# A two-block transformer kernel on one core: w_ada's chunks dealt anew between TensorE and VectorE, filler multiplications of a constant tile in three pauses, and the attention's quotient moved behind its last product

## The reference

```
mod = silu(c) @ w_ada + b_ada                       # 2048 x 12288, one row
shift_a, scale_a, gate_a, shift_f, scale_f, gate_f = split(mod, 6)
h = rms_norm(x, g_attn_pre) * (1 + scale_a) + shift_a
proj = h @ w_in                                     # 2048 x 5456
diff = (softmax(q1 k1) - lam * softmax(q2 k2)) v, then rms_norm     # 8 heads
dsa  = softmax over each query's 64 best keys, chosen by an indexer # 8 heads
x = x + gate_a * rms_norm(concat(diff, dsa) @ w_o, g_attn_post)
h = rms_norm(x, g_ffn_pre) * (1 + scale_f) + shift_f
x = x + gate_f * rms_norm((silu(h @ w_gate) * (h @ w_up)) @ w_down, g_ffn_post)
# second block: latent attention and a gated convolution on w_in_2, then
x = x + rms_norm(merged @ w_out_2, post_norm_g_2)
```

## Time and profile before

| | us |
|---|---|
| median of 3 executions | 2359.15 (2357.89 to 2360.88) |
| profiled execution | 2358.56 |
| its span in the trace | 2357.3 |
| PE busy | 2279.3 (97%) |
| DVE busy | 1401.9 (59%) |
| ACT busy | 1070.8 (45%) |
| mean DMA rate | 215 GB/s |

### The profile page before, as it was taken

One profiled execution on the slowest core, in us unless ns is written; L12 is line 12 of the kernel. 1 busy time (PEld: TensorE's weight loads), 2 busy tenths in 40 slices (PEclk: granted clock), 3 DMA queues, 4 the chain that ended last, 5 costly groups with the idle time before them and its releaser, 6 DMA issues.

```text
span 2357.3 us, 26193 instructions
## 1 busy us (share of the span) xinstructions
PE 2279.3 (97%) x10706; PEld 1843.9 (78%) x10706; DVE 1401.9 (59%) x1902; ACT 1070.8 (45%) x1481; POOL 0.7 (0%) x5
## 2 busy tenths in 40 slices
PE   6989899989999999999999999999999999999998
PEld 3666677778888888888887878888888888888887
DVE  3669999786774555455456554545544554554555
ACT  2424455544434444434445555555444444444443
POOL 0000000000000000000000000000000000000000
PEclk9999999999999999999999999999999999999999
DMA  9887667665775665555553644444555555555553
GB/s 401 342 349 290 261 259 283 242 252 194 290 276 203 220 226 192 183 196 196 181 194 113 249 153 156 158 159 164 187 192 194 191 184 196 183 192 195 181 192 146
DMA packets 79548, 507.77 MB, mean 215 GB/s; under 512 B 8364, under 2 KB 18860, under 8 KB 19780
## 3 DMA queue, kind: packets, MB, share of 16 engines
q1 hardware_dynamic: 79428, 506.10, 58.5%
HBM read 501.87 MB, written 4.19 MB: 215 GB/s over the span
## 4 chain that ended last, share of the span: by engine, by line
PE 88%; DVE 6%; ACT 2%; DMA 2%; issue 1%; SPq 0%; DVEq 0%; ACTq 0%
PE bank L611 27%; PE bank L613 27%; PE bank L612 27%; DMA raw<-in_chunks_dram 2%; PE bank L656 1%; DVE wlo L1787 1%; PE bank L741 1%; DVE acc L1768 1%; PE bank L575 1%; ACT whi L1133 1%; PE bank L664 1%; PE bank L764 0%; DVE P L1946 0%; PE bank L744 0%; DVE x L1848 0%
## 5 line engine op out<-in xcount | busy, mean ns | idle before, releaser
L1787 DVE TENSOR_TENSOR wlo<-raw,whi 128x1024 fp32r<-128x1024 f32 (+2 forms) x760 | 912.5, 1204 | 837.6 <-ACT whi L1133 836.2
L1133 ACT ACTIVATE whi<-raw 128x1024 fp32r<-128x1024 f32 (+2 forms) x760 | 790.0, 1044 | 1002.2 <-PE bank L613 910.4
L611 PE MATMUL bank<-whi,Ahi 128*128 128x512 f32 (+2 forms) x2304 | 909.0, 395 | 31.1 <-DVE wlo L1787 21.0
L613 PE MATMUL bank<-whi,Alo 128*128 128x512 f32 (+2 forms) x2304 | 893.8, 388 | 0.0
L612 PE MATMUL bank<-wlo,Ahi 128*128 128x512 f32 (+2 forms) x2304 | 893.7, 388 | 0.0
L611 PEld LDWEIGHTS bank<-whi,Ahi 128*128 128x128 f32 x2304 | 435.5, 189 | 138.0 <-DVE wlo L1787 31.3
L613 PEld LDWEIGHTS bank<-whi,Alo 128*128 128x128 f32 x2304 | 435.4, 189 | 89.4
L612 PEld LDWEIGHTS bank<-wlo,Ahi 128*128 128x128 f32 x2304 | 436.1, 189 | 82.3
L1768 DVE SCALAR_TENSOR_TENSOR acc<-raw,cs,acc 128x512 f32<-128x512 f32 x224 | 157.4, 744 | 0.1
L611 PE MATMUL bank<-whi,Fhi 128*128 128x512 f32 x352 | 137.6, 391 | 0.0
L613 PE MATMUL bank<-whi,Flo 128*128 128x512 f32 x352 | 137.1, 389 | 0.0
(11 more groups left out here) (292 smaller groups left out, 1336.9 us busy)
## 6 DMA issues: line engine op xcount, KB each, us to landing
raw<-in_chunks_dram SPq DMA_DIRECT2D x456, 1024.0 KB, 4.8
raw<-in_chunks_dram SPq DMA_DIRECT2D x8, 768.0 KB, 4.2
raw<-in_chunks_dram SPq DMA_DIRECT2D x8, 576.0 KB, 4.1
raw<-in_chunks_dram SPq DMA_DIRECT2D x4, 672.0 KB, 8.1
x<-in_x_turned_dram SPq DMA_DIRECT2D x2, 1024.0 KB, 10.3
x<-in_x_dram SPq DMA_DIRECT2D x4, 512.0 KB, 5.8
x_spill<-x SPq DMA_DIRECT2D x2, 1024.0 KB, 9.7
x<-x_spill SPq DMA_DIRECT2D x2, 1024.0 KB, 8.9
```

The source lines that it names most:

```text
L611: pe.matmul(o, a_hi, w_hi, start=beg and kk == 0, stop=False)
L613: ins = pe.matmul(o, a_lo, w_hi, start=False, stop=fin and kk == 1)
L1133: act.activation(m.whi[:, i % NHL, :, 0:n], m.raw[:, c % NRAW, 2 * h:2 * h + 2, 0:n], ACT.Copy).then_inc(m.s_hi, 1)
L1787: dve.tensor_tensor(m.wlo[:, i % NHL, :, 0:n], m.raw[:, c % NRAW, 2 * h:2 * h + 2, 0:n], m.whi[:, i % NHL, :, 0:n].bitcast(F32), ALU.subtr ...
```

## The change

It has four parts. (1) `ADA_ON_PE` loses groups 1, 2 and 3, the shifts of quarters 1 to 3; VectorE multiplies them, at the head of its own list. TensorE has 20 chunks, VectorE 60 up to the end of `w_o`. (2) The deal: TensorE's chunks follow the first two passes of each of three quarters; VectorE's are spread over all quarters, and `W_IN_HALF` sets how many fall in each half of `W_IN_ORDER`. The shift of the next quarter now comes by `ada_take` in bank 5; banks 6 and 7 alternate for the scales. `idle` is only set after quarter 2. (3) `keep_busy(b, n)` multiplies a tile of ones with the constants, 440 columns, n times, into a bank that nobody reads: at the start, and in both `turn_halves`, ahead of each wait. (4) `combine` makes `E1 - lam * s1 / s2 * E2`, and ScalarE multiplies with 1 / s1 as it copies the product out, in one instruction for each half of the positions.

```diff
--- before.py
+++ after.py
@@ -38,15 +38,16 @@
 W_IN_ORDER = (4, 6, 1, 3, 5, 7)
 
 
-DEAL_PE = ((3, 3, 2, 2, 1), (2, 2, 1, 1, 1), (2, 2, 2, 0, 0), (0, 0, 0, 0, 0))
-DEAL_VECTOR = ((0, 0, 0, 0, 0), (0, 0, 0, 1, 1), (0, 0, 0, 1, 1), (1, 1, 1, 1, 2))
-W_IN_SHARE = 24
+DEAL_PE = ((2, 2, 0, 0, 0), (2, 2, 0, 0, 0), (2, 2, 0, 0, 0), (0, 0, 0, 0, 0))
+DEAL_VECTOR = ((0, 2, 2, 1, 1), (0, 1, 1, 1, 1), (0, 1, 1, 1, 1), (1, 0, 1, 1, 1))
+
+W_IN_HALF, W_IN_SHARE = 11, 25
 W_O_SHARE = 15
 THIRDS = ((0, 4), (4, 8), (8, 11))
 
 
 
-ADA_ON_PE = (4, 0, 5, 1, 6, 2, 7, 3)
+ADA_ON_PE = (4, 0, 5, 6, 7)
 
 
 def win_cols(cg):
@@ -61,7 +62,7 @@
         plan.append(("lin", w, k0, c0, n))
 
     first = [("ada", g, j) for g in ADA_ON_PE for j in range(4)]
-    rest = [("ada", g, j) for g in range(8, 20) for j in range(4)]
+    rest = [("ada", g, j) for g in (1, 2, 3, *range(8, 20)) for j in range(4)]
     plan += first[:8]
     del first[:8]
     for q in range(4):
@@ -79,7 +80,12 @@
         nonlocal n
         n += 1
         m = 4 * len(W_IN_ORDER)
-        due = n * W_IN_SHARE // m if n <= m else W_IN_SHARE + -(-(n - m) * (late - W_IN_SHARE) // W_O_SHARE)
+        if n <= m // 2:
+            due = n * W_IN_HALF // (m // 2)
+        elif n <= m:
+            due = W_IN_HALF + (n - m // 2) * (W_IN_SHARE - W_IN_HALF) // (m // 2)
+        else:
+            due = W_IN_SHARE + -(-(n - m) * (late - W_IN_SHARE) // W_O_SHARE)
         while rest and late - len(rest) < due:
             plan.append(rest.pop(0))
 
@@ -592,7 +598,6 @@
         yield
 
     k = Walk()
-    k.idle = idle
 
     def linear(w, c0, n, operand, ready, ks=(0, 4, 8, 12), kbase=0, s=None, begin=True, end=True, before=None, skew=False):
 
@@ -665,11 +670,19 @@
         ins.then_inc(m.filled[b], 1)
         return b, n
 
-    def turn_halves(src, ready, scaled):
+    def keep_busy(b, n):
+
+        need.wait_ge(m.freed[b], k.uses[b])
+        for _ in range(n):
+            pe.matmul(m.bank[b][:, 0:NCONST], m.ones, m.const[:, :], start=True, stop=True)
+
+    def turn_halves(src, ready, scaled, fill):
+
 
         for b in (4, 5):
             need.wait_ge(m.freed[b], k.use(b) - 1)
         for tb in range(2):
+            keep_busy(6, fill[tb])
             need.wait_ge(*ready[tb])
             for b in (4, 5):
                 for kk in range(2):
@@ -709,6 +722,8 @@
             ins.then_inc(m.filled[4], 1)
         if (idx, j) == (1, 2):
             ada_columns(0)
+        if idx == 1 and j < 3:
+            keep_busy(5, 1)
 
     def shifted(base):
 
@@ -720,12 +735,14 @@
     need.wait_ge(m.s_cs, 1)
     ada_products(0, 8, beside)
     ada_columns(1)
+    keep_busy(5, 3)
     for q, cg in WIN_ITEMS[:3 * len(W_IN_FIRST)]:
         first_part(q, cg)
         if cg == W_IN_FIRST[2]:
-            ada_columns(2 * q + 2)
+            ada_columns(q + 2)
         if cg == W_IN_FIRST[3]:
-            ada_columns(2 * q + 3)
+            ada_take(k.take(), 5)
+    k.idle = idle
 
 
 
@@ -934,7 +951,7 @@
 
 
 
-    turn_halves(x_block, [(m.s_diag, 1), (m.s_diag, 2)], True)
+    turn_halves(x_block, [(m.s_diag, 1), (m.s_diag, 2)], True, (5, 2))
     F_at = {}
 
     def ff_turn(kf, s):
@@ -976,7 +993,7 @@
         A_at[q] = [turn_block(4 + j, x_block, 4 * q + 2 * j) for j in range(2)]
 
     A_ready = operand_at(A_at)
-    A_at[0] = turn_halves(x_block, [(m.s_xp, 9), (m.s_xp, 13)], False)
+    A_at[0] = turn_halves(x_block, [(m.s_xp, 9), (m.s_xp, 13)], False, (0, 3))
     linear("w_in_2", B_QA, 512, m.A_op, A_ready, before=lambda j: k.soon(block2_operand, j + 1) if j < 3 else None)
     linear("w_in_2", B_KV, 288, m.A_op, A_ready)
     linear("w_in_2", B_KV + 288, 288, m.A_op, A_ready)
@@ -1210,11 +1226,14 @@
 
     def first_operand(q):
 
-        k.use(6)
-        shift_at = k.use(7)
+        k.use(6 if q == 0 else 6 + (q + 1) % 2)
+        if q:
+            k.take()
+        b = 5 if q else 7
+        shift_at = k.use(b)
         for j in range(2):
             need.wait_ge(m.s_t, 2 * q + j + 1)
-            need.wait_ge(m.freed[7], shift_at)
+            need.wait_ge(m.freed[b], shift_at)
             for kk in (2 * j, 2 * j + 1):
                 kb = 4 * q + kk
                 ins = act.activation(m.Ahi[:, kb, :], m.tmpA[:, q % 2, kk, :], ACT.Identity, bias=m.modT[:, kb:kb + 1])
@@ -1244,13 +1263,12 @@
     for q, cg in WIN_ITEMS[:3 * len(W_IN_FIRST)]:
         first_part(q, cg)
         if cg == W_IN_FIRST[1]:
-            gather(2 * q + 2)
-        if cg == W_IN_FIRST[2]:
-            gather(2 * q + 3)
+            gather(q + 2)
         if cg == W_IN_FIRST[3]:
             first_operand(q + 1)
         if (q, cg) == WIN_ITEMS[2]:
             tables()
+    k.idle = idle
 
 
 
@@ -1357,7 +1375,13 @@
         def finish(h, pv):
             b = ln.bank[1]
             c0 = C_DQ + 128 * h
-            copy_out(m.P1[:, :, c0:c0 + 128], b, pv, m.bank[b][:, 0:256].rearrange("p (t d) -> p t d", t=2))
+            need.wait_ge(m.filled[b], pv)
+            for tb in range(2):
+                ins = act.activation(m.P1[:, tb, c0:c0 + 128], m.bank[b][:, 128 * tb:128 * tb + 128], ACT.Copy,
+                                     scale=ln.sm[:, (h - lo) % 2, 1, 2 * tb:2 * tb + 1])
+                if tb == 0:
+                    a.up(ins)
+            ins.then_inc(m.freed[b], 1)
             need.wait_ge(m.freed[b], pv)
             for tb in range(2):
                 need.wait_ge(m.s_a, a.n)
@@ -1892,8 +1915,9 @@
 
     def first_scale(q):
 
-        k.use(6)
-        mod(ADA_ON_PE[2 * q], 6, k.use(6))
+        b = 6 if q == 0 else 6 + (q + 1) % 2
+        k.use(b)
+        mod(4 + q, b, k.use(b))
         released(mod_at[4 + q])
         ks = slice(4 * q, 4 * q + 4)
         v.up(dve.scalar_tensor_tensor(out=m.gs[:, ks], in0=m.modT[:, 16 + 4 * q:20 + 4 * q], scalar=1.0,
@@ -1914,10 +1938,12 @@
 
     def first_shift(q):
 
-        k.use(7)
-        mod(ADA_ON_PE[2 * q + 1], 7, k.use(7))
         if q == 0:
+            k.use(7)
+            mod(0, 7, k.use(7))
             k.split_to(UNIT_AT[LIN[1]])
+        else:
+            mod(k.groups[k.take()], 5, k.use(5))
         released(mod_at[q])
         need.wait_ge(m.s_t, 2 * q + 2)
         settle()
@@ -2182,14 +2209,15 @@
 
         def combine(slot, sc):
 
+
             sm = inverse(ln, slot, sc)
             inv = sm[:, 1, :].rearrange("p (t m) -> p t m", m=2)[:, :, 1]
-            v.up(dve.tensor_scalar(sm[:, 0, 0:2], inv, m.lam[:, 1:2], None, ALU.mult))
+            total = sm[:, 3, :].rearrange("p (t m) -> p t m", m=2)[:, :, 0]
+            v.up(dve.scalar_tensor_tensor(out=sm[:, 0, 0:2], in0=inv, scalar=m.lam[:, 1:2], in1=total,
+                                          op0=ALU.mult, op1=ALU.mult))
             settle()
             for tb in range(2):
                 e1, e2 = (ln.Ex[:, 0:256], ln.Ex[:, 384:640]) if tb else (ln.Ex[:, 256:384], ln.Ex[:, 640:768])
-                v.up(dve.tensor_scalar(e1, e1, sm[:, 1, 2 * tb:2 * tb + 1], None, ALU.mult))
-                settle()
                 ins = dve.scalar_tensor_tensor(out=e1, in0=e2, scalar=sm[:, 0, tb:tb + 1], in1=e1,
                                                op0=ALU.mult, op1=ALU.add)
                 if tb == 0:
```

## The result

The change makes the kernel slower: 2365.51 us (median of 9 runs, 2364.25 to 2367.47) against 2360.84 us for the kernel before in 9 runs (2357.89 to 2363.73). The ratio is 1.0021, with a 95% interval of 1.0012 to 1.0029. Forecast were 2346.0 us and a fall; the time lies above the range.

What follows compares the result with a forecast made beforehand. Transfers were taken to bound 33 to 147 us, then DVE and PE by turns, PE from 440 us on. Terms of -7, -4, +1, +2 and -4.5 us summed to -12.5: 2358.56 to 2346.0 us, range 2335 to 2357.

Steps and rivals of the forecast that it cites:

- 33 to 147 us, "no gain": Quarters 0, 1 and half of 2, taken as bound by transfers: no gain, between +5 and -5 us.
- the lost PE products and the two transfers give back: Quarters 1 and 2: ring refill costs some 5 us each, offset by fewer PE products and two fewer transfers.
- 147 to 203 us: End of the quarters, DVE-bound: two chunks fewer save 5.3 us; -7 us taken together with the stretch before.
- the last addition: Sign of being right: the quarters' last addition near 195 us and not 202; at or past 202 us, wrong.
- 203 to 303 us: After the quarters: mostly one DVE chunk fewer (2.65 us) and four heads' shorter quotient (2.9 us); -4 us, ends 0 and -6.
- 303 to 400 us, "+1": Two more DVE chunks, 5.3 us, into 10.3 us of idle time: +1 us, ends 0 and +5.
- 400 to 510 us, "+2": `w_o` stretch: three more DVE chunks, 8.0 us and an addition, mostly into idle time: +2 us, ends 0 and +8.
- waits for `wlo` of over 8 us: Sign of being wrong: PE waits for `wlo` of over 8 us from 400 us on.
- The pauses, "-4.5": Pauses at 510 and 1266 us: fillers save slow matmuls and slow turns, 2.6 and 2.3 us; -4.5 us taken.
- if the clock is up, which it is when they begin: Both pauses: the condition under which the fillers cost nothing; at half clock they would delay the turns by 6 us.
- DVE becomes the bound from the first quarter on; slower: Rival, quarters 0 to 2: 12 us of the added DVE work lies on the path; about 2364 us, chance 0.08.
- The rival of new pauses that drop the clock: Rival, near 50 and 70 us: PE without `wlo` loses its clock, some 2 us each; 2352.5 us, chance 0.11.

Runs made afterwards that it cites:

- a2: Changed kernel with the three moved shift groups multiplied on VectorE in 32 of 512 columns from their third row block on; 2358.18 us, ratio 0.9990.
- c1: Changed kernel with 22 in place of 18 VectorE chunks in the quarters, later stages dealt as in the kernel before; 2369.97 us, ratio 1.0035.
- d2: c3 with two VectorE chunks fewer in the last quarter, put into the rest of w_in and into w_o; 2354.53 us, ratio 0.9975.
- a1: Changed kernel without any fillers, neither at the start nor in the two pauses; 2368.87 us, ratio 1.0033.
- a4: Changed kernel with a third set of fillers behind the second turns, three in the first pause and two in the second; 2364.05 us, ratio 1.0015.
- b3: Kernel before, old dealing, with the new quotient and all pause fillers, the third ones too; 2355.34 us, ratio 0.9977.
- c3: b3 with only the last quarter's shift group moved to VectorE, its four chunks inside quarters 1 to 3; 2353.02 us, ratio 0.9962.
- c4: b3 with the change's six fillers at the start added; 2355.59 us, ratio 0.9978.
- d1: Like c3, but with two shift groups on VectorE, those of quarters 2 and 3; 2364.36 us, ratio 1.0016.
- c2: Changed kernel with the rotary tables computed after the third pass of quarter 1 instead of in quarter 0; 2365.84 us, ratio 1.0021.

## Why the prediction was wrong

The forecast was a sum of -12.5 us; the traces have +8.4. The step that failed, in three of its terms, is that added chunks fit into DVE's idle time as a window counts it. Taken were "no gain" up to 147 us, +1 from 303 and +2 from 400 us; the traces have +5.6, +7.1 and +6.3. The other large miss is the pauses, -4.5 taken and -0.5 in the traces. Against the sum, the stretches up to 203 us miss by 5.5 us, those from 303 to 510 us by 10.4, the pauses by 4.0 and 203 to 303 us by 1.0.

*33 to 147 us, "no gain": wrong.* The walk along DVE's queue held: the tables run 3.85 us late (69.13 in place of 65.28 us; I said about 3), and the second pass of quarter 1 begins 4.6 us late by its `wlo` (number 12; I said about 4 for the end of the first). What failed is the sentence that in quarters 1 and 2 "the lost PE products and the two transfers give back" what the burst costs. The stretch ends 5.6 us late. I read 57 us of idle DVE over 114 us, and missed where it lies. Of the 23.4 us in 33 to 75 us, 15.1 lie ahead of 54 us, where `whi` comes late, and the burst comes behind that. A shorter window alone would not have told it: in 54 to 90 us DVE had 16.3 us of idle time before, and its work grew by 12.2. What decides is the order in the queue, since each `wlo` stands behind the chunks. PE has little to gain from lighter work there. At number 10 the arithmetic of the moved chunks is 4.3 of the 6.6 us (a2 against the changed kernel); the rest, the order of chunks and transfers among it, no run takes apart. By number 28 a2 shows the two sides apart: I had set some 10 us of relief (PE's products and two transfers) against 9 us of burst (4 in quarter 0, then 5), and the relief is 3.6 us, the burst 9.2.

*147 to 203 us: near in size.* Two chunks fewer were to give 5.3 us; the trace has 7.1. But as -7 was meant for both stretches, the sum of the two came out at -1.5 us. Row for row: the last addition at 200.85 and not near 195 us, which the prediction had named as a sign of being right. DVE was busy for 79.7 of 114 us up to 147 us, 70% where the sign was over 80%.

*203 to 303 us: right,* -3.0 us by the trace against -4, with the quotient at 1.4 to 1.7 us of it and not 2.9.

*303 to 400 us, "+1": mis-sized,* +7.1. I had set two chunks against 10.3 us of idle DVE time in 97 us and took it that they would fit. The five added chunks from 303 us on stand against 7.1 + 6.3 = 13.4 us, 2.7 us each, of which the slow matmuls at 408.60 us are 0.5; c1 gives 2.5 and d2 2.6. The idle time that a window counts on DVE was no room. The trace of the kernel after has a second cost at the start of the stretch that no count of chunks has. PE comes back from a wait for the exponentials at the low clock:

```profile
299.26 0.78 PE L616 MATMUL bank<-whi,Ahi 128*128 128x512 f32 x1
...
304.10 0.63 PE L618 MATMUL bank<-whi,Alo 128*128 128x512 f32 x1
```

Twelve matmuls run slow here, behind number 64, against six in the kernel before (303.15 to 305.9 us), which has twelve more ahead of that wait, from 293.16 us. A gate group's 512-column sums (2.1 us) also fall into this place, where the kernel before has a group's four columns (0.95). No experiment took this apart.

*400 to 510 us, "+2": mis-sized,* +6.3, near its bad end of +8. The sign that I had named, waits for `wlo` of over 8 us from 400 us on, didn't come: the list of waits has two for `wlo`, 0.9 us in all. Some 3.5 us of the 6.3 are the longer wait at 408.60 us (3.80 in place of 2.74) and the clock's fall behind it, which the sum had no term for.

*The pauses, "-4.5": wrong in the traces (-0.5), nearer in the medians* (3.4 us between a1 and the changed kernel, 2.8 by the ratios, of which the traces place 2.2 in the pauses). The error is mostly one step: "if the clock is up, which it is when they begin". It was up, through fillers and turns, and fell in the 2.87 us behind them, which I had left in the row before as "issue" without asking what PE would do there. And 1.0 us that I had booked for the faster second turns was never on the path, as a `wlo` on DVE covers them. a4 and b3 show the fall undone when that gap is filled; even then the traces give 3.0 us over both pauses in a4 against the kernel before, not 4.5. The five first fillers were to end at 513.9 us, as the turns could begin; they end 3.9 us after they begin, at the moment that the diagonal tile is there.

*The rivals.* "DVE becomes the bound from the first quarter on; slower", at 2364 us and a chance of 0.08, is what happened in size and, up to 400 us, in its split: +7 to 147 us (measured +5.6), -5.3 to 203 us (-7.1), -2 to 303 us (-3.0), +5 to 400 us (+7.1), +5 in `w_o` (+6.3), -4.5 for the pauses (-0.5). Its terms add up to +5.2 us, where the traces have +8.4 and the medians 4.7, so that its 2364 us lies so near the 2365.51 is luck in part. The rival of new pauses that drop the clock happened as well, inside it: 0.81 in 54 to 90 us, and the fall behind 408.60 us.

*The dealing by itself.* By the medians the fillers give 3.4 us and the quotient 2.5 in the changed kernel, so that the dealing costs some 4.7 + 3.4 + 2.5 = 10.6 us; by the ratios it is 9.9. The direct comparison in one batch, a4 with b3, says 8.7 us.

*What stays open.* Why two groups cost so much more than one is shown only as far as the places go (7.6 us by number 10, in quarter 0, and 6.1 us between numbers 18 and 28). Whether one group's gain could be had without pushing seven chunks into the last quarter wasn't tried beyond d2. And why the clock falls behind a pause with the same fillers and idle time in one kernel and not in another, and for eight matmuls in one and twelve in another, no run explains.

## What to carry to other kernels

Before work is moved into an engine's idle time, ask where in the order of instructions that time lies and what is queued behind the moved work. An idle share over 100 us told nothing about the 36 us that mattered, and even in those 36 us the counted idle time was larger than the added work. Relief for an engine that waits for the loaded one was worth little here (3.6 us of 12). An added chunk cost most or all of its 2.65 us in the last quarter and from 303 us on. One moved group was faster than none by the medians where three lost, so try the small step first. A clock kept up by fillers must be kept up to the first real matmul, the gap behind the last turn included.

## What the runs showed of the hardware

With fillers up to the last gap and PE idle for 0.65 us (first pause) and 0.19 us (second) in front of the first matmul, the granted clock stayed at 1.00 in all twelve pauses of six kernels (a4, b3, c3, c4, d1, d2). With the same fillers but idle times of 2.87 and 1.67 us left there, it fell to 0.50, the level of 1.2 GHz, in twelve of sixteen pauses of eight kernels. The same fillers and the same idle time went with a fall in one kernel and with none in another: c2 and the changed kernel both idle for 1.67 us in the second pause, and only the changed kernel has matmuls at steps of 0.43 us behind it.

The fall does not show where one looks for it. In the changed kernel the clock was 1.00 up to the first matmul of the first pause, 0.51 behind it, and I had taken the clock at the end of the fillers for the clock at the first matmul. In its second pause the fall came two matmuls after PE had resumed at its full rate (1280.38, then steps of 0.43 us from 1281.28 us). In c2's first pause it came ahead of the first matmul: 528.26 us by the record of the clock, where the matmul begins at 529.31.
